# One barrier between stages: semaphores made once and handed on in a single-core hybrid encoder step

## What is computed

```python
def trunk(x, q_pos, caches, params):
    for l in range(DEPTH):                      # DEPTH = 2
        h = rmsnorm(x, g_mix[l])
        if l % 2 == 0:                          # even: A = top-k indexed attention, B = latent attention
            y, rows = even_mixer(h, ...)
        else:                                   # odd: C = forgetting attention, D = stick-breaking attention
            y, rows = odd_mixer(h, ...)
        x = x + y
        y, new_buf = conv_ffn(rmsnorm(x, g_ffn[l]), buf, w_up[l], w_conv[l], b_conv[l], w_down[l])
        x = x + y
    out = rmsnorm(x, g_final)
```

## Time and profile before

| what | us |
|---|---|
| median of 3 runs | 3221.77 (3221.39 to 3222.02) |
| the profiled execution, its time | 3223.93 |
| its span in the trace | 3221.7 |
| PE busy in it | 2981.9 (93%) |
| DVE, ACT, POOL busy in it | 1729.8, 1278.0, 168.5 |

### The profile page before, as it was taken

How to read it: one execution, slowest core, us unless ns; L and a number is a source line. 1 busy time by engine, 2 the same in 40 slices (tenths; PEclk the granted TensorE clock), 3 DMA queues, 4 the chain that set the end, 5 groups by cost and what they waited for, 6 DMA issues and landing times. The chain is left out here.

```text
span 3221.7 us, 48872 instructions
## 1 busy us (share of the span) xinstructions
PE 2981.9 (93%) x17421; PEld 2530.4 (79%) x17421; DVE 1729.8 (54%) x3768; ACT 1278.0 (40%) x2682; POOL 168.5 (5%) x240
## 2 busy tenths in 40 slices
PE   8976885998999999999899798988889999999998
PEld 6752553677999999999799467855679999999998
DVE  5447998754444445544431664158654444445545
ACT  4435994543222222222243454357532222222223
POOL 0000222310000000000000330000000000000000
PEclk9996997999999999999999799999999999999999
DMA  4110001021111111111311201110201111111112
GB/s 144 54 49 0 14 13 46 1 77 48 48 39 52 39 39 52 39 39 52 130 48 49 79 2 63 55 56 1 77 11 55 39 39 52 39 39 52 39 40 75
DMA packets 146190, 151.98 MB, mean 47 GB/s; under 512 B 17116, under 2 KB 122196, under 8 KB 146068
## 3 DMA queue, kind: packets, MB, share of 16 engines
q1 hardware_dynamic: 146068, 150.44, 15.2%
HBM read 126.65 MB, written 23.24 MB: 47 GB/s over the span
## 5 line engine op out<-in xcount | busy, mean ns | idle before, releaser
L223 PE MATMUL ffn_up<-hlow_r,ffn_uhi 128*128 128x384 f32 (+1 forms) x2112 | 691.1, 327 | 0.0
L2161 DVE SCALAR_TENSOR_TENSOR ffn_cv<-ffn_G,ffn_ctap,ffn_cv 128x256 f32<-128x256 f32 (+1 forms) x352 | 168.8, 500 | 493.3 <-ACT ffn_cv L2087 488.7
L223 PEld LDWEIGHTS ffn_up<-hlow_r,ffn_uhi 128*128 128x128 f32 x2112 | 398.6, 189 | 0.9
L2081 ACT ACTIVATE ffn_G<-ffn_up 128x384 f32<-128x384 f32 (+2 forms) x176 | 65.2, 397 | 825.1 <-PE ffn_up L224 825.1
L2194 DVE TENSOR_TENSOR xres<-ffn_dn,xres 128x512 f32<-128x512 f32 (+1 forms) x396 | 263.6, 687 | 132.3 <-PE ffn_dn L224 121.1
L222 PE MATMUL ffn_dn<-ffn_dhi,ffn_ahi 128*128 128x512 f32 x704 | 280.7, 399 | 2.9
L224 PE MATMUL ffn_dn<-ffn_dhi,ffn_alo 128*128 128x512 f32 x704 | 278.3, 395 | 0.0
L223 PE MATMUL ffn_dn<-ffn_dlo_r,ffn_ahi 128*128 128x512 f32 x704 | 278.3, 395 | 0.0
L222 PE MATMUL ffn_up<-mixed_c_r,ffn_uhi 128*128 128x384 f32 (+1 forms) x528 | 174.9, 331 | 5.9 <-DVE ulo_r L2138 5.9
L222 PE MATMUL ffn_up<-mixed_a_r,ffn_uhi 128*128 128x384 f32 (+1 forms) x528 | 174.6, 331 | 5.7 <-DVE ulo_r L2138 5.7
L222 PE MATMUL ffn_up<-mixed_d_r,ffn_uhi 128*128 128x384 f32 (+1 forms) x528 | 174.3, 330 | 0.0
(11 more groups left out here) (473 smaller groups left out, 6944.2 us busy)
## 6 DMA issues: line engine op xcount, KB each, us to landing
ulo<-in_w_up_dram SPq DMA_DIRECT2D x44, 512.0 KB, 5.0
ffn_ulo<-in_w_up_dram SPq DMA_DIRECT2D x44, 512.0 KB, 4.6
ffn_dlo<-in_w_down_dram SPq DMA_DIRECT2D x22, 1024.0 KB, 4.9
w_d<-in_w_in_odd_dram SPq DMA_DIRECT2D x7, 768.0 KB, 10.3
proj_even_x<-in_x_prompt_dram SPq DMA_DIRECT2D x8, 512.0 KB, 3.4
xres<-in_x_prompt_dram SPq DMA_DIRECT2D x8, 512.0 KB, 4.5
scratch_x<-xres SPq DMA_DIRECT2D x8, 512.0 KB, 3.5
x_d<-scratch_x SPq DMA_DIRECT2D x8, 512.0 KB, 3.9
```

What stands on the lines that cost most here:

```text
L223: nc.tensor.matmul(out, lh, rl, start=False, stop=False)
L2081: s.activation(G[:, g0:g0 + w], upbank(c, b, 0)[:, j:j + w], ACT.Copy).then_inc(g_out, 1)
L2161: last = v.scalar_tensor_tensor(cv[:, 0, j:j + w], G[:, g0 - 2 + tapno:g0 - 2 + tapno + w], ctap[:, c, tapno:tapno + 1], cv[:, 0, j:j + w] ...
```

## The change

All 84 stage semaphores (`SEMAPHORES`) and the 18 that reach over stages (`SHARED`) are made once at the start. A stage takes its semaphores off the front of a list, `Phase.free`. When it has ended, the next stage gives the job of setting them back to one engine, POOL or SP (`reset_by`), which does it in its own stream ahead of its part of the stage, while the other engines go into the stage at once; after that they go to the end of the list. The block `start` is left in the first stage only, where the four engines set back the first stage's semaphores as before; POOL then sets all others for the first time. SP does it in the four attention stages and in `forget`, POOL in the other seven. The shared semaphores are set once and never again.

```diff
 class Phase:
+    free = []
+    last = []
-    def __init__(self, nc, name):
-        self.nc, self.name, self.ctx, self.sems = nc, name, ExitStack(), []
+    def __init__(self, nc, name, reset_by="pool"):
+        self.nc, self.name, self.ctx, self.sems, self.reset_by = nc, name, ExitStack(), [], reset_by
...
     def __exit__(self, *a):
+        Phase.last = self.sems
         return self.ctx.__exit__(*a)
...
     def sem(self, name):
-        s = self.ctx.enter_context(self.nc.semaphore(f"{self.name}_{name}"))
-        self.sems.append(s)
-        return s
+        self.sems.append(Phase.free.pop(0))
+        return self.sems[-1]
 
     def block(self):
-        def reset(eng, share):
-            for s in self.sems[share::4]:
+        def reset(eng, sems):
+            for s in sems:
                 eng.sem_clear(s)
                 eng.sem_inc(s, FROM)
 
-        with self.nc.Block() as start:
-            @start.sync
-            def _(sp):
-                reset(sp, 0)
...
+        eng = self.nc.gpsimd if self.reset_by == "pool" else self.nc.sync
+        if Phase.unset:
+            with self.nc.Block() as start:
+                @start.sync
+                def _(sp):
+                    reset(sp, self.sems[0::4])
...
+            reset(eng, [s for s in Phase.unset if s not in self.sems])
+            Phase.unset = []
+        reset(eng, Phase.last)
+        Phase.free += Phase.last
+        Phase.last = []
         return self.ctx.enter_context(self.nc.Block())
+
+    @staticmethod
+    def provide(nc, ctx):
+        Phase.free = [ctx.enter_context(nc.semaphore(f"stage_sem{j}")) for j in range(SEMAPHORES)]
+        shared = {x: ctx.enter_context(nc.semaphore(x)) for x in SHARED}
+        Phase.unset, Phase.last = Phase.free + list(shared.values()), []
+        return shared
...
-    with Phase(nc, f"att_{kind}") as ph:
+    with Phase(nc, f"att_{kind}", "sync") as ph:
         sb, sem = ph.sb, ph.sem
-        if fetch is not None:
-            ph.sems += fetch.sems
...
-    with Phase(nc, "forget") as ph:
+    with Phase(nc, "forget", "sync") as ph:
```

More of the change, by code:

```diff
@@ L63, in sem, with _ @@
     def sem(self, name):
-        s = self.ctx.enter_context(self.nc.semaphore(f"{self.name}_{name}"))
-        self.sems.append(s)
-        return s
+        self.sems.append(Phase.free.pop(0))
+        return self.sems[-1]
     def block(self):
-        def reset(eng, share):
-            for s in self.sems[share::4]:
+        def reset(eng, sems):
+            for s in sems:
                 eng.sem_clear(s)
                 eng.sem_inc(s, FROM)
-        with self.nc.Block() as start:
-            @start.sync
-            def _(sp):
-                reset(sp, 0)
[L79 to L89, removed]
-        return self.ctx.enter_context(self.nc.Block())
+        eng = self.nc.gpsimd if self.reset_by == "pool" else self.nc.sync
[4 more added lines that the diff above has]
+                    reset(sp, self.sems[0::4])
+                @start.tensor
+                def _(pe):
+                    reset(pe, self.sems[1::4])
+                @start.vector
+                def _(dve):
+                    reset(dve, self.sems[2::4])
+                @start.scalar
+                def _(act):
+                    reset(act, self.sems[3::4])
+            reset(eng, [s for s in Phase.unset if s not in self.sems])
[3 more added lines that the diff above has]
+        Phase.last = []
+        return self.ctx.enter_context(self.nc.Block())
+    @staticmethod
[4 more added lines that the diff above has]
+        return shared
+SEMAPHORES = 84
+SHARED = ([f"{w}_{x}" for w in ("wo_even", "w_c", "w_d", "wo_odd") for x in ("soon_in", "late_in", "x_in")] +
+          [f"{x}_in{s}" for x in ("q", "wkv", "raw") for s in range(2)])
 def bc(ap, n):
@@ L244, with __init__ @@
 class Ahead:
-    def __init__(self, nc, ctx, name, w_dram, homes, low, late=(), pairs=False, x=None):
+    def __init__(self, shared, name, w_dram, homes, low, late=(), pairs=False, x=None):
         self.w_dram, self.homes, self.low, self.late, self.pairs, self.x = w_dram, homes, low, late, pairs, x
@@ L251, in __init__ @@
         self.order = self.soon + list(late) + [FAR]
[L252 to L255, removed]
+        self.soon_in, self.late_in, self.x_in = (shared[f"{name}_{x}"]
+                                        for x in ("soon_in", "late_in", "x_in"))
     def rows_of(self, k):
@@ L1514, in index_scores @@
         set_up = sem("set_up")
-        ph.sems += soon["sems"]
         block = ph.block()
@@ L1747, in output_projection @@
         sb, sem = ph.sb, ph.sem
-        ph.sems += nxt["sems"]
         whi = sb("whi", [P, KD, D], F32R)
@@ L2243, in hybrid_step @@
     with ExitStack() as ctx:
+        shared = Phase.provide(nc, ctx)
         def sb(name, shape, dt=F32):
@@ L2264, in ffn_state @@
                    "taps": [tensor(ff, f"tap{layer}", [P, 4 * NF]), tensor(ff, f"st{layer}", [P, 2 * NF])],
-                   "raw_in": ff.enter_context(nc.semaphore(f"raw_in{layer}"))}
-            nxt["sems"] = [nxt["raw_in"]]
+                   "raw_in": shared[f"raw_in{layer}"]}
             return xres, hlow, nxt
@@ L2288, in hybrid_step @@
                         "wkv": [tensor(both, f"wkv{s}", [P, 2 * P]) for s in range(2)],
-                        "q_in": [both.enter_context(nc.semaphore(f"q_in{s}")) for s in range(2)],
-                        "w_in": [both.enter_context(nc.semaphore(f"w_in{s}")) for s in range(2)]}
-                soon["sems"] = soon["q_in"] + soon["w_in"]
+                        "q_in": [shared[f"q_in{s}"] for s in range(2)],
+                        "w_in": [shared[f"wkv_in{s}"] for s in range(2)]}
                 index_scores(nc, dram, consts, src, soon)
@@ L2295, in hybrid_step @@
             mixed_a = twin(nc, far, "mixed_a", [P, 4, TOK], side="right")
-            pre = Ahead(nc, wo, "wo_even", dram["w_o_even"][0], *homes(wo, "wo_even", D), pairs=True)
+            pre = Ahead(shared, "wo_even", dram["w_o_even"][0], *homes(wo, "wo_even", D), pairs=True)
             attention(nc, dram, consts, "a", src, mixed_a[0], pre)
@@ L2306, in hybrid_step @@
               for r in range(2)]
-        pre = Ahead(nc, far, "w_c", w_odd[:, 0:C_IN], *wc, late=range(FAR - 4, FAR), x=tensor(far, "x_c", [P, D], side="right"))
+        pre = Ahead(shared, "w_c", w_odd[:, 0:C_IN], *wc, late=range(FAR - 4, FAR), x=tensor(far, "x_c", [P, D], side="right"))
         conv_ffn(nc, dram, consts, 0, xres, (mixed_a[1], mixed_b[1], hlow[1]), nxt, out, x1, pre)
@@ L2325, in hybrid_step @@
                     mixed_c = twin(nc, near, "mixed_c", [P, 4, TOK], side="right")
-                    pre = Ahead(nc, wd, "w_d", w_odd[:, C_IN:C_IN + D_IN], *homes(wd, "w_d", D_IN),
+                    pre = Ahead(shared, "w_d", w_odd[:, C_IN:C_IN + D_IN], *homes(wd, "w_d", D_IN),
                                 x=tensor(wd, "x_d", [P, D], side="right"))
@@ L2331, in hybrid_step @@
                     mixed_d = twin(nc, near, "mixed_d", [P, 4, TOK], side="right")
-                    pre = Ahead(nc, wo, "wo_odd", dram["w_o_odd"][0], *homes(wo, "wo_odd", D))
+                    pre = Ahead(shared, "wo_odd", dram["w_o_odd"][0], *homes(wo, "wo_odd", D))
                     attention(nc, dram, consts, kind, src, mixed_d[0], pre)
```

## The result

| | median, us | runs, from and to |
|---|---|---|
| before, measured with it | 3221.89 | 4, 3221.39 to 3222.53 |
| after | 3198.78 | 4, 3195.79 to 3201.62 |
| ratio | 0.9926 | 95%: 0.9911 to 0.9941 |
| profiled execution after: time, span, mean granted clock | 3197.15, 3195.4, 0.965 | before: 3223.93, 3221.7, 0.960 |

It is faster by 23 us where 16 were forecast; the 3198.8 lies under the low end of the range, 3201. That makes 22.0 us the better figure for the gain, uncertain by about 0.9 (the standard errors of the two means are 0.8 and 0.2): 16.1 forecast and 6 more.

What follows compares the result with a forecast made beforehand. PE, busy 93% of the span, was taken to bound the kernel; removing 16.1 us of gaps between stages, with added clears hidden and nothing for the clock, gave a median of 3205.7 us, range 3201 to 3210.

Steps and rivals of the forecast that it cites:

- What is removed: Start block gone at 12 stage boundaries: PE's clears 11.8 us, fixed parts 4.0, late DVE about 0.3; 16.1 us taken away.
- the fixed part: Branches, drain, gather and release in each boundary's gap, beside PE's clears: taken as 0.33 us, 4.0 us over 12.
- What is added: The same clears on POOL (0.1 us each) or SP (0.08) beside the next stage, all hidden: no cost.
- rival 1: Start block covered code fetching; each of 12 stages now begins with a 0.4 us stop: 4.8 us back, 3210.5 us, chance 0.13.
- The clock: PE's low clock behind gaps at the two `ffn` stages: 6 us more gained or 3 lost; nothing taken.
- Rival 2: Shorter idle time spares PE low clock at the two `ffn` stages: up to 6 us, say 4; 3201.7 us, chance 0.12.
- Waits inside a stage keep their lengths: All engines and DMAs start each stage earlier by the same gap, so nothing inside a stage changes length.
- what would prove it wrong: Stage ends set by POOL or SP, first waits growing as gaps shrink, or stages changing by more than 1 us each.
- The range: 3201 to 3210 us, to hold 8 in 10; the forecast's own range was 3203 to 3208.5.

Runs made afterwards that it cites:

- filled kernel: Changed kernel plus identity transposes on PE where it would wait at stage starts and ends: median 3192.5 us; with gaps put back 3210.5, with doubled gaps 3226.1.
- bare barrier: Changed kernel with an empty all-engine block, no clears, ahead of each of the 12 later stages: median 3206.2 us, ratio 0.9954 to the old kernel.
- repeats of before: Old kernel run twice more without an edit, for two more traces: 3221.9 and 3220.6 us, eight runs each.
- gaps back: Changed kernel with a block ahead of each later stage in which PE clears a spare semaphore as often as it cleared there before: median 3221.2 us, ratio 0.9998.

## Why the prediction was wrong, point by point

- **What is removed: right.** 16.1 us of gaps were forecast from the earlier trace rows, 16.1 is what the releases say, and 33.2 for 33.7 us in the filled kernels shows that a gap's length is its direct price. The bare barrier is 0.33 us between releases at nine of twelve boundaries, as the fixed part was taken by the earlier trace rows; three late engines bring the mean to 5.0 / 12 = 0.42.
- **What is added: right.** 49 clears on POOL into `index` took 229.7 to 235.1, 0.11 us each where 0.1 was taken, and the fills of `bias` stand behind them (POOL's clears, then its timeline, after):

```profile
L75 POOLq EVENT_SEMAPHORE_RANGE_CLEAR  x49: 44/44/44, 229.7 to 235.1; - x49
```

```profile
235.23 0.42 POOL L1565 MEMSET bias<- 128x384 bf16 x1 [234.78 <-issue]
235.70 0.23 POOL L1569 MEMSET bias<- 64x64 bf16 x2
235.99 0.36 POOL L1571 MEMSET bias<- 64x320 bf16 x1
```

  `index` kept its 61.18 us. In `forget` SP's 32 clears were over 0.6 us ahead of the store (clears, then timeline, after; to the earlier trace rows), and the stage is 0.7 us shorter:

```profile
L75 SPq EVENT_SEMAPHORE_RANGE_CLEAR  x32: 25/25/30, 1766.6 to 1768.8; - x32
```

```profile
1769.38 0.40 SPq L1659 DMA_DIRECT2D out_p_c_logf_dram<-forget_u  x1
```

- **Code to be fetched (rival 1): not seen.** The first instructions of PE, DVE and ACT stand as far behind the release as before in each of the 12 later stages (within 0.05 us; in `att_c` DVE and ACT are 0.4 us earlier): in `out_0` PE's first weight load 2.81 us, DVE 0.80 and ACT 0.14 in both traces. The Trainium skill ("Runtime: NRT & Kernel Launch", Instruction fetch mechanics) has a taken branch to code that isn't at hand stop the engine; each stage begins with one, as it did before, and the branch costs no more now that no start block stands ahead of it. Stops like the one on DVE in the earlier trace rows do come: in the bare barriers above one engine was 0.3 to 0.5 us late at three of twelve boundaries. What they are, code or something else, no run shows.
- **The clock: the step that failed.** The prediction says "I take nothing and keep both ends"; the runs show some 6 us of gain there by the means, 10.2 inside the stages in the profiled pair. It had the ends, 6 us of gain and 3 of loss, from the two `ffn` starts alone. `ffn_up` at the start of `ffn_0`, windows, after:

```profile
787.80:793.80 6.00, 6.00 (x22) 6.00 (x23) 0.00 (x0) 0.00 (x0) 0.62 1.10 364
793.80:799.80 6.00, 6.00 (x36) 6.00 (x36) 0.00 (x0) 0.49 (x1) 1.00 0.83 337
```

  0.62 and 22 matmuls where there were 0.50 and 19: `ffn_0` won 0.9 us and `ffn_1` 0.1. The rest came in stages that the clock paragraph didn't look at: `att_b` 3.7, `att_d` 2.9, `proj_d` 1.4, `att_c` 1.3, `proj_c` 1.0; `proj_even` lost 2.0 in this pair, which the repeats of before show to be chance. They show the same for the gains of `proj_c` (175.3 and 176.9 in them) and of `ffn_0` (805.1 in both); those of `att_b`, `att_c`, `proj_d` and `att_d` stand against all three traces of before. Rival 2 (less idle time spares PE low clock) had the mechanism and about the size, 4 us for a measured 6, and the wrong place. In the filled kernel the two `ffn` stages do give 4.3 us, so their starts were a place to gain, but shorter gaps alone didn't reach it. The chance of 0.12 was too low: the mean granted clock under 1 at every kind of boundary, 0.50 to 0.84, was there to be read in windows before.
- **"Waits inside a stage keep their lengths": not so.** A stage of the same instructions starts with the clock in another state and goes through it at another speed. The prediction named this itself as what would prove it wrong, stages that change by over 1 us; five did (`att_b`, `att_d`, `proj_even`, `proj_d`, `att_c`), and the last stage starts 26.2 us earlier, not 16.
- **The range.** Its low end of 3201 allowed 5 us for the clock and nothing for the runs' own spread. The runs known then lay within 0.6 us; 71 runs of the same kernel lie within 9.

How much a low stretch costs cannot be read from its length alone. The mean clocks give the time at 1.2 GHz as (1 - clock) / 0.5 of the span: 258 us before, 224 after, 172 filled. The Trainium skill ("TensorE: Matmul & The Clock Gate", Terms) puts the penalty at the throttled time times the share of pulses held back, here one half; that gives an estimate of 17 us less for after and 43 for the filled kernel. The stages shrank by 10.2 and 15.3. The trace shows one reason why the rule is an upper end here: before, in the 4 us from 226 on, the clock is at 0.50 throughout, but PE is busy for 1.57 of them.

**Open:** which property of a boundary sets where the next low stretches fall. The surplus was 1.7, 5.2 and 3.1 us for gaps of 5, 16 and 31 us. `att_d` had its short form with the gaps back too (164.5), and `att_b` its long one with a bare barrier of 0.33 us ahead of it (242.9): by single stages the low stretches don't follow the gap's length. Moving single stages by fractions of a microsecond with the gaps unchanged was not tried.

## What to carry to other kernels

Price idle time between stages in two terms: its length, which a list of clears and barriers gives to 0.1 us, and the clock behind it, for which windows of the granted clock must be read at every boundary and deep into the next stage. Before a range is drawn from one profile, run the old kernel often enough to see its own spread. Where PE waits at a stage's ends, some idle transposes into a free bank are cheap: here they brought 6.5 to 8.7 us on top of the change.

## What the runs showed of the hardware that was not expected

- A clear on POOL is spaced 0.11 us ((235.1 - 229.7) / 48), between ACT's 0.10 and DVE's 0.13.
- An empty all-engine barrier costs 0.33 us from release to release at nine boundaries and 0.59 to 0.79 at three, where one engine came late; 5.0 us over 12.
- One program on one core takes 3217.5 to 3226.5 us, and single stages of it differ by up to 2.7 us between executions, with the granted clock at 1.00 or 0.50 for the same matmuls.
- With PE busier at the boundaries, 16.0 us of gaps cost 16.8 us; without, 15.8 us cost 21.0.
- Transposes of the identity can hold the granted clock at 1.00: the 85 behind `att_b` in the filled kernel are all that PE does from 511.4 to 520.9; in after PE has nothing to do there. Windows, columns as above, filled and then after:

```profile
511.36:520.86 9.50, 9.50 (x89) 9.26 (x85) 9.33 (x13) 0.00 (x0) 0.00 (x0) 1.00 0.00 0
```

```profile
512.40:529.00 16.60, 0.00 (x0) 0.00 (x0) 16.18 (x23) 0.00 (x0) 0.00 (x0) 0.50 0.00 0
```
